# Routed experts in a new order, their first bias on two partitions, rotary scores grouped

## The reference

```python
q_l = jnp.concatenate([q_l[..., :B_NOPE], apply_rope(q_l[..., B_NOPE:], cos, sin)], axis=-1)
k_l = [k_nope, broadcast(k_pe)]
logits = jnp.einsum('bqhd,bkhd->bhqk', q_b, k_all) * scale
p = jax.nn.softmax(logits, axis=-1)
```

```python
logits = xt @ w_router + b_router
top_v, top_e = lax.top_k(logits, TOP_K)
gates = jax.nn.softmax(top_v, axis=-1)
# for each padded block of an expert's tokens:
clamped_swiglu(xb @ w1[e] + b1[e]) @ w2[e] + b2[e]
# rows are weighted by their gates and added up per token
```

## Time and profile before

| | |
|---|---|
| median of 3 runs | 2593.35 us (2586.8 to 2596.13) |
| the profiled execution | 2588.46 us, span 2586.7 us |
| mean granted TensorE clock | 0.976 |
| PE busy | 2430.8 us (94%) |
| DVE, ACT busy | 929.2 us (36%), 640.4 us (25%) |
| DMA | 568.00 MB, mean 220 GB/s |
| L2366, first products of the experts | 2304 records, 511.5 us busy |
| L2390, second products | 1152 records, 255.1 us busy |
| L2358, first bias | 288 records, 69.6 us busy |

### The profile page before, as it was taken

How to read it: one execution, slowest core, us unless ns; L and a number is a source line. 1 busy time by engine, 2 the same in 40 slices (tenths; PEclk the granted TensorE clock), 3 DMA queues, 4 the chain that set the end, 5 groups by cost and what they waited for, 6 DMA issues and landing times. The chain is left out here.

```text
span 2586.7 us, 31850 instructions
## 1 busy us (share of the span) xinstructions
PE 2430.8 (94%) x11962; PEld 1296.1 (50%) x11963; DVE 929.2 (36%) x2118; ACT 640.4 (25%) x1479; POOL 46.8 (2%) x57
## 2 busy tenths in 40 slices
PE   6999999999999998899899789999999999999997
PEld 4545675457644567676786553333333233333222
DVE  2107624043610583427354433232232233233223
ACT  3016623332311253326331321111111111111111
POOL 0000000000100000100001000000000000000000
PEclk9999999999999998899999799999999999999999
DMA  8117921200211102339341149977999986999997
GB/s 294 66 67 273 350 102 45 81 32 1 98 65 52 47 1 85 111 122 328 105 140 56 64 181 365 378 321 287 418 418 418 417 338 271 417 418 418 418 418 295
DMA packets 154190, 568.00 MB, mean 220 GB/s; under 512 B 10800, under 2 KB 12336, under 8 KB 121040
## 3 DMA queue, kind: packets, MB, share of 16 engines
q1 hardware_dynamic: 154096, 566.72, 56.0%
HBM read 565.64 MB, written 1.05 MB: 219 GB/s over the span
## 5 line engine op out<-in xcount | busy, mean ns | idle before, releaser
L2366 PE MATMUL PS<-BIG,PW 128*64 128x512 f32 x2304 | 511.5, 597 | 15.4 <-DMA BIG<-in_w 15.4
L2366 PEld LDWEIGHTS PS<-BIG,PW 128*64 128x64 f32 x2304 | 159.6, 137 | 364.8 <-issue 316.0
L2390 PE MATMUL PS<-BIG,PW 128*64 128x512 f32 x1152 | 255.1, 595 | 8.6 <-ACT PW L2462 8.6
L2522 DVE TENSOR_SCALAR PW<-PS 128x512 f32<-128x512 f32 x36 | 24.9, 691 | 558.8 <-PE PS L2366 558.8
L2459 ACT ACTIVATE PW<-PW 128x512 f32<-128x512 f32 x36 | 22.7, 630 | 795.6 <-DVE PW L2522 795.6
L2390 PEld LDWEIGHTS PS<-BIG,PW 128*64 128x64 f32 x1152 | 79.2, 137 | 161.4 <-issue 144.3
L883 PE MATMUL PS<-HT,BIG 128*128 128x512 f32 (+1 forms) x448 | 154.7, 504 | 0.0
L557 PE MATMUL PS<-HT,BIG 128*128 128x256 f32 x640 | 139.5, 379 | 2.1 <-PEq L666 2.1
L557 PEld LDWEIGHTS PS<-HT,BIG 128*128 128x128 f32 x640 | 121.4, 190 | 19.0 <-issue 2.7
L883 PEld LDWEIGHTS PS<-HT,BIG 128*128 128x128 f32 x448 | 86.2, 192 | 62.7 <-issue 56.9
L1181 PE MATMUL PS<-BIG,HT 128*128 128x512 f32 x256 | 110.0, 592 | 0.0
(11 more groups left out here) (436 smaller groups left out, 3193.3 us busy)
## 6 DMA issues: line engine op xcount, KB each, us to landing
BIG<-in_w SPq DMA_DIRECT2D x384, 1024.0 KB, 14.7
BIG<-in_l_w_ada SPq DMA_DIRECT2D x24, 2048.0 KB, 8.4
BIG<-in_l_w_in SPq DMA_DIRECT2D x20, 2048.0 KB, 8.0
BIG<-in_w_ada SPq DMA_DIRECT2D x12, 2048.0 KB, 8.0
BIG<-in_l_w_out SPq DMA_DIRECT2D x8, 2048.0 KB, 8.9
BIG<-in_w_in SPq DMA_DIRECT2D x7, 2048.0 KB, 9.1
BIG<-in_w_out SPq DMA_DIRECT2D x2, 2048.0 KB, 8.0
BIG<-in_l_w_in SPq DMA_DIRECT2D x1, 1792.0 KB, 10.6
```

The costliest lines, as they stand in the source:

```text
L2366: ins = nc.tensor.matmul(PS[64 * g:64 * g + 64, 4 + half, :], xt[:, c % 4, c // 4, :], W[:, c, half * F + g * 512:half * F + g * 512 + 512 ...
L2390: ins = nc.tensor.matmul(PS[64 * g:64 * g + 64, 7, :], at_[:, k % 4, k // 4, :], W[:, 8 + k // 2, k % 2 * D + g * 512:k % 2 * D + g * 512 ...
```

## The change

1. `attention` gets `parts`; the latent layer's `score` makes its full-array products for both heads first and then both 64-row products. The other two callers make one product a call, as before.
2. `bias1` has its two halves on partitions 0 and 32; the load writes two rows of 4 KB where it wrote one of 8 KB, and the four bias products take the halves alternately.
3. Experts are worked off by a key. An expert with more than one block is heavy, one with one block light; with nH and nL of them the i-th heavy one has the key (i - 0.75) nL, the j-th light one (j - 0.5) nH, expert 0 a key below all. DVE makes for each pair of experts whether one is later than the other, PE sums that into each expert's first block and rank.
4. Routing order: the 64-wide gain products go (ACT copies `gain_split` from the 128-wide ones, two copies of 64 partitions), half of the rest moves behind the counts, and the 32 records of the residual's transposes move from the routing to behind the second gather of the first block.

```diff
@@ attention, scores
-                        for h in range(2):
-                            ins = score(h, units[i], slice(a, b), PS[:, 2 * (i % 2) + h, a:b])
+                        for part in range(parts):
+                            for h in range(2):
+                                ins = score(h, units[i], slice(a, b), PS[:, 2 * (i % 2) + h, a:b], part)
@@ latent layer
-                nc.tensor.matmul(out, qn[:, head, q], kn[:, head, k], start=True, stop=False)
+                if part == 0:
+                    return nc.tensor.matmul(out, qn[:, head, q], kn[:, head, k], start=True, stop=False)
                 return nc.tensor.matmul(out, qr[half, u[0], q], kpe[half, k], start=False, stop=True)
@@ routed_experts
+            def load_bias1(sp, e):
+                sp.dma_start(bias1[0:64:32, :], t["b1_2"][e, :].rearrange("o (h f) -> (o h) f", h=2)).then_inc(bias_landed, 16)
@@ routing, ACT
-                    nc.scalar.copy(gain_split, PS[:, 4, :])
                     for g in range(2):
+                        nc.scalar.copy(gain_split[64 * g:64 * g + 64, :], PS[64 * g:64 * g + 64, 6 + g, :])
                         nc.scalar.copy(gain_rows[:, g * 512:g * 512 + 512], PS[:, 6 + g, :])
@@ routing, PE
-                    for k in range(KT):
+                    def turn_gain(k):
                         column = modulation(4)[:, 5 * KT + k, :]
                         at_g = slice(k % 4 * P, k % 4 * P + P)
-                        nc.tensor.matmul(PS[64 * (k // 4):64 * (k // 4) + 64, 4, at_g], column.to_broadcast([P, 64]), ident, start=True, stop=True)
-                        ins = nc.tensor.matmul(PS[:, 6 + k // 4, at_g], column.to_broadcast([P, P]), ident, start=True, stop=True)
-                    ins.then_inc(S["transposed"].sem, 1)
+                        return nc.tensor.matmul(PS[:, 6 + k // 4, at_g], column.to_broadcast([P, P]), ident, start=True, stop=True)
+
+                    for k in range(KT // 2):
+                        turn_gain(k)
...
-                    for n in range(4):
-                        pe.wait_ge(*at("d_ready", n + 1))
-                        for j in range(4):
-                            nc.tensor.matmul(PS[:, n, j * P:(j + 1) * P], XT[:, n % 2 * 4 + j, n // 2 * P:(n // 2 + 1) * P], ident,
-                                             start=(j == 0), stop=False, skip_group_check=True)
+                    for k in range(KT // 2, KT):
+                        ins = turn_gain(k)
+                    ins.then_inc(S["transposed"].sem, 1)
+
+                    pe.wait_ge(*at("ranked", 1))
+                    nc.tensor.matmul(PS[:, 5, 3 * E:5 * E], ones[0:E, :], flat(later[0:E, :, :]), start=True, stop=True).then_inc(
+                        S["order_ready"].sem, 1)
@@ routing, DVE, after the block counts
-                    link(nc.vector.tensor_tensor_scan(pend, ones[:, 0:E], blocks, 0.0, ALU.mult, ALU.add))
-                    link(tt(tmp, pend, blocks, ALU.subtract))
+                    stt = nc.vector.scalar_tensor_tensor
+                    link(ts(some, blocks, 1.0, None, ALU.min))
+                    link(ts(heavy, blocks, 1.5, None, ALU.is_gt))
+                    link(tt(light, some, heavy, ALU.subtract))
+                    link(nc.vector.tensor_tensor_scan(heavy_rank, ones[:, 0:E], heavy, 0.0, ALU.mult, ALU.add))
+                    link(nc.vector.tensor_tensor_scan(light_rank, ones[:, 0:E], light, 0.0, ALU.mult, ALU.add))
+                    link(ts(tmp, heavy_rank, -0.75, light_rank[:, E - 1:E], ALU.add, ALU.mult))
+                    link(ts(key, light_rank, -0.5, heavy_rank[:, E - 1:E], ALU.add, ALU.mult))
+                    link(nc.vector.copy_predicated(key, heavy.bitcast(U32), tmp))
+                    link(stt(key, key, 128.0, const("expert_row"), ALU.mult, ALU.add))
+                    link(nc.vector.memset(key[:, 0:1], -1000.0))
+                    for x, y in ((key, key_of), (blocks, blocks_of), (some, some_of)):
+                        link(stt(own, x, 1.0, ident[:, 0:E], ALU.mult, ALU.mult, accum_out=y))
+                    link(ts(later[:, 0, :], key, key_of, blocks_of, ALU.is_gt, ALU.mult))
+                    ts(later[:, 1, :], key, key_of, some_of, ALU.is_gt, ALU.mult).then_inc(S["ranked"].sem, 1)
+                    dve.wait_ge(*at("order_ready", 1))
+                    link(nc.vector.tensor_copy(tmp, PS[:, 5, 3 * E:4 * E]))
+                    link(nc.vector.tensor_copy(rank, PS[:, 5, 4 * E:5 * E]))
+                    link(tt(pend, tmp, blocks, ALU.add))
@@ loop, PE, first_products
-                        for half in range(2):
-                            for g in range(2):
-                                ins = nc.tensor.matmul(PS[64 * g:64 * g + 64, 4 + half, :], ones[0:1, 0:SLOT],
-                                                       bias1[0:1, half * F + g * 512:half * F + g * 512 + 512], start=True, stop=False)
+                        for g in range(2):
+                            for half in range(2):
+                                row = slice(32 * half, 32 * half + 1)
+                                ins = nc.tensor.matmul(PS[64 * g:64 * g + 64, 4 + half, :], ones[row, 0:SLOT],
+                                                       bias1[row, g * 512:g * 512 + 512], start=True, stop=False)
@@ first block of the loop, PE
                     gather_next(0)
+                    for n in range(4):
+                        for j in range(4):
+                            nc.tensor.matmul(PS[:, n, j * P:(j + 1) * P], XT[:, n % 2 * 4 + j, n // 2 * P:(n // 2 + 1) * P], ident,
+                                             start=(j == 0), stop=False, skip_group_check=True)
                     pe.wait_ge(loop["gates_copied"], 1)
@@ plan, DVE
-                    link(ts(some, blocks, 1.0, None, ALU.min))
-                    link(nc.vector.tensor_tensor_scan(rank, ones[:, 0:E], some, 0.0, ALU.mult, ALU.add))
-                    for n, (x, y) in enumerate(((pend, some), (rank, ones[:, 0:E]), (rank, blocks))):
-                        link(nc.vector.scalar_tensor_tensor(scratch, x, const("partition"), y, ALU.is_le, ALU.mult,
-                                                            accum_out=plan_by[:, n:n + 1]))
-                    link(ts(plan_by[:, 1:2], plan_by[:, 1:2], float(E - 1), None, ALU.min))
+                    link(stt(scratch, pend, const("partition"), some, ALU.is_le, ALU.mult, accum_out=plan_by[:, 0:1]))
+                    link(nc.vector.tensor_tensor(tmp, some, const("expert_row"), ALU.mult))
+                    link(stt(scratch, rank, const("partition"), tmp, ALU.is_equal, ALU.mult, accum_out=plan_by[:, 1:2]))
+                    link(stt(scratch, rank, const("partition"), blocks, ALU.is_lt, ALU.mult, accum_out=plan_by[:, 2:3]))
                     link(ts(plan_by[:, 2:3], plan_by[:, 2:3], -1.0, 0.0, ALU.add, ALU.max))
-                    link(nc.vector.tensor_copy(plan_by[:, 3:4], pend[:, E - 1:E]))
-                    nc.vector.tensor_copy(plan_by[:, 4:5], rank[:, E - 1:E]).then_inc(loop["plan_ready"], 1)
+                    link(nc.vector.tensor_reduce(plan_by[:, 3:4], blocks, AX, ALU.add))
+                    nc.vector.tensor_reduce(plan_by[:, 4:5], some, AX, ALU.add).then_inc(loop["plan_ready"], 1)
```

More of the change, by code:

```diff
@@ L276, in layers_and_experts_kernel @@
                  "square_sum_ready rms_ready inverse_ready rstd_ready scaled_ready tile_ready tile_taken rope_mixed rope_taken "
-                 "scores_ready max_ready exp_ready scores_used probs_ready probs_turned turned_copied heads_ready "
+                 "ranked order_ready scores_ready max_ready exp_ready scores_used probs_ready probs_turned turned_copied heads_ready "
                  "heads_taken rows_copied columns_ready columns_taken h_ready normed_ready residual_ready a_ready b_ready c_ready d_ready e_ready f_ready g_ready i_ready j_ready k_ready").split()
@@ L638, in rope_turn, with attention @@
             dve_chain.link(dve, nc.vector.tensor_tensor(x[:, 0:LAT], x[:, 0:LAT], tmp, ALU.add))
-        def attention(units, scale, score, value, mask_of, sink, gate, together=True, mods=None):
+        def attention(units, scale, score, value, mask_of, sink, gate, together=True, mods=None, parts=1):
             probs = PW[:, 0:2048].rearrange("p (b h k) -> p b h k", b=2, h=2)
@@ L914, in window_layer, with score @@
             ws.done = first + 5
-            def score(h, u, k, out):
+            def score(h, u, k, out, part):
                 half = slice(64 * h, 64 * h + 64)
@@ L1083, in latent_layer @@
             units += [(m, q, [2, 3]) for m in range(4) for q in (2, 3)]
-            attention(units, (nope + rot) ** -0.5, score, value, lambda u: None, None, gate, together=False)
+            attention(units, (nope + rot) ** -0.5, score, value, lambda u: None, None, gate, together=False, parts=2)
             project_out(1, HT, 2)
@@ L2165, in routed_experts @@
             htok = take(BIG, rest, 2, D)
```

(18 more changed lines are left out.)

## The result

The changed kernel takes 2557.03 us (median of four runs, 2552.02 to 2558.71) where the kernel before takes 2594.69 (four runs, 2586.8 to 2596.13): ratio 0.9858, 95% interval 0.9833 to 0.9882, so 31 to 43 us faster. The profiled executions are 2556.34 and 2588.46 us, 32.1 apart where the medians are 37.7 apart: the kernel before spreads over 9 us from one execution to the next.

A forecast was written before the change was run, and what follows sets the result against it. Both stages were taken to run at PE's pace, with weight DMA a close second limit in the expert loop. Terms -24.4 - 16.6 + 4.6 = -36.4 gave 2552.1 (profiled) or 2557.0 (median); forecast 2555, range 2540 to 2580 us.

The forecast's parts named there:

- Part 1, order and bias: Expert loop: new expert order and shorter bias group together, -24.4 us; order alone or bias alone -13 each.
- the bias group: Four bias products per expert block: 0.93 us instead of 1.86, all overlapping; 36 blocks give -33.5 us of PE work.
- The bias load: Expert bias load as two rows of 4 KB: taken as 0, bounds -7 to +7 us; two engines would give some -4.
- Rival (e): Expert weight loads: bias load over two partitions drains the queue, 2.2 us more a load, near 2609 us; chance 0.03.
- Part 2, scores: Latent layer's attention: grouped rotary scores save 1.25 and 0.83 us a unit, eight units of each, -16.6 us.
- rival b: Latent attention: softmax binds once PE is faster, part 2 worth nothing, about 2571 us; chance 0.08.
- Part 3, the start: Routing to first expert blocks: chain 0, moved transposes +1.6, low clock +3, together +4.6 us.
- The chain: Router's products to first gather: earlier counts offset the added ranking operations, net 0, bounds -1 to +3 us.
- the clock: Gather, its transposes and start of first products run at half clock after PE idles: +3 us, bounds 0 and +5.
- rival (c): Start of expert loop: low clock well into first products and longer ranking chain, +8 us, about 2563; chance 0.08.
- (a): Expert loop's bias group: the four products do not all overlap, 1.86 us stays, about 2566 us; chance 0.12.
- (d): Expert loop's order: does not help, as if the doubles stood as before, part 1 -13, about 2566 us; chance 0.05.

The follow-up runs named there:

- the same with the new spacing: Changed kernel with the residual transposes back in the routing and keys putting the doubles at 7, 13, 19 and 25: 2538.4 us.
- The two runs with the products of the identity: Transposes-in-routing run plus 15 unread identity products in PE's idle stretches before the first gather: 2555.85 us; with doubles at 7, 13, 19, 25 too: 2540.14 us.

## Why the prediction was right

**Forecast 2555, measured 2557.03**, in the range; against the profiled execution 2552.1 forecast and 2556.34 measured. The medians lie closer than the sum deserves: the 36.4 us forecast stand against 37.7 between the medians, but 32.2 between the spans, where the stages can be checked.

**Part 1, order and bias.** Forecast -24.4; from block 2 on -21.0 came where -22.5 was forecast. The account held block by block: three stretches, three paced blocks at the end of each, none behind the last double, 30.42 us a paced block. Two details of it were off: the third paced block is the first block of the double and not a single, and the issues behind the doubles lie 57.6 us apart once and 51.7 three times, where 53.6 had been given for all four. The waits rose, as forecast (21.1 us of PE's gaps; 30.8 us if each paced block is counted by its excess over 26.88, forecast 31.8). The term that was off is the bias group: 0.93 assumed, 1.02 measured. Per block 0.09 us, 36 blocks: 3.2 us of PE work, of which by the account 1.1 reach the end, the rest being time that PE would have waited. The other 0.4 us lie in the waits: with a group of 1.02 the account gives 29.5 us of them, and 30.8 were measured. The runs also bear out the -13 that the prediction gave for order or bias alone: from block 2 on, order alone (the run with the old bias) takes 12.4 us less than before, and bias alone (the old order) 10.1, with the two groups ahead 11.8. By the rows, the four bias products are 3.4 times as fast as four groups of two records one behind the other (4 x 0.86 us, an estimate from the 0.43 us of a record). The Trainium skill has 3.07 for four row tiles ("TensorE: Matmul & The Clock Gate", Part 3). The prediction's estimate of 1.2 us from that factor starts from its own 0.93; from 4 x 0.86 it would be 1.12. The measured 1.02 lies below either.

**The bias load.** Nothing to see in the pace: 30.42 to 30.49 before, 30.42 to 30.43 after, 30.44 to 30.51 with the old load put back. The 64 more packets fit the Trainium skill's rule in "DMA: Bandwidth & Descriptors" (how many engines a DMA uses) that two rows go to two engines, but no view here shows which engines moved them. The 4 us that I had estimated from it did not come. Rival (e), the queue drained by the load, has no trace at all; its price was also added up too high, since 24 x 2.2 is 53 and not 54, which would have ended 16 us above before.

**Part 2, scores.** -16.4 for -16.6. Softmax did not take over (rival b): the idle time of PE on DVE's products in the whole attention is unchanged, 0.98 us at each of the last two units.

**Part 3, the start.** The chain came out at -0.2 for 0. The counts do start 4.8 us earlier behind the router (9.4 us for 14.3), and the ranking takes that back. What lies behind was sized by the wrong neighbour. The row of the router gave 6.8 us of half clock and I took 3 us; here it lasts 20.5 us, from 1513.9 to 1534.4. At 1.2 GHz PE takes 3.68 us for the gather (1.94 at full clock), and the first products, whose first 5 us lie in the stretch, take 16.46 (13.95). First gather to second gather is 24.2 us for 19.4, +4.9; as the bias group in it is 0.84 shorter, the clock costs 5.7 us where 3 were forecast, more than the bound of 5. The low clock of rival (c) did come, at less than its price. The moved transposes cost +1.4 (1545.72 to 1552.86 against 1555.74 to 1561.53), as forecast (+1.6). But in the kernel before, the clock fell once more at 1577.0 and block 1's first products took 15.65 us, which I had read and not put into the sum; after the change they take 13.95. That is 1.7 us which no term of the sum held, and luck that it fell against the clock's 2.7. Net +3.7 for +2.7:

```profile
1521.79 3.68 PE L2364 MATMUL PS<-BIG,HT 128*64 128x512 f32 x8 [4.96 <-DVE HT L2518]
...
1529.33 16.46 PE L2397 MATMUL PS<-BIG,PW 128*64 128x512 f32 x64
...
1547.91 3.84 PE L2441 MATMUL PS<-CONST,XT 128*128 128x128 f32 x32
...
1566.50 13.95 PE L2397 MATMUL PS<-BIG,PW 128*64 128x512 f32 x64
```

**Rivals** (a) and (d) are settled: the bias group is 1.02 us and the doubles stand where the keys put them. Taken back, the bias gives 2570 and the order 2566 (both had been priced at 2566).

## What to carry to other kernels

Where an engine's time and a transfer's time per item are close, draw up both limits item by item, with the lead that the buffers can hold; shares and sums of waits hide that the same saving is worth 8.6 us in one order and 12.3 in another, and the order itself nearly 60 (from 2542 to 2600 us with the same work). Put items that give the transfer time (here experts with two blocks) where the lead is just used up, not evenly: of the orders run here the best has seven singles ahead of the first double, where the start gives a lead of its own, and five between doubles. Small products whose inputs and outputs both leave room are worth placing on different input rows as well as different output halves, and products of one shape should follow each other.

## What the runs showed of the hardware

Four products with one input row each, on two input partitions 32 apart and two output halves, took 1.02 us where two at a time took 1.86; the order among the four did not matter (1.02 us either way).

The half clock at the start of the expert loop does not follow PE's idle time alone. With the same order of PE's instructions and only other keys the fall ahead of the gather lasted 13.6 us (the transposes in the routing, change's order) or 3.4 us (the same with the new spacing, 1518.8 to 1522.2). PE in order of time there, the gather, and the first products of block 1, which run over the second fall:

```profile
1519.49 3.29 PE L2369 MATMUL PS<-BIG,HT 128*64 128x512 f32 x8 [4.96 <-DVE HT L2519]
...
1557.45 1.09 PE L2394 MATMUL PS<-BIG,CONST 1*64 1x512 f32 x8 [1.73 <-DVE HT L2586]
1558.46 15.65 PE L2402 MATMUL PS<-BIG,PW 128*64 128x512 f32 x64
```

In the first case the clock fell once more, at 1548.7, in the second twice, at 1559.8 and 1576.9, so that router to block 2 took 95.8 and 94.6 us. At 1576.9 PE had had no idle time since 1557.45; in the kernel before it fell at 1577.0, and the last idle time, 1.73 us, was that before 1574.12. The two runs with the products of the identity repeat this, 13.6 us and some 3.4. In the first case PE was busy for 12.10 of the 13.60 us at 0.50 (the window above). The low clock moved and got shorter but was not removed by any of the runs, and from the router to block 2 the changed kernel and these four take 94.6 to 95.9 us, where the kernel before takes 92.3. What sets the low clock was not found.
